# Adding the two halves of an up tile on VectorE alone, in the feed-forward stages of a two-block transformer kernel

## The reference

```python
D_MODEL, D_FF, SEQ, CONV_W = 1024, 2816, 256, 3

def conv_ffn(x, w_up, conv_w, w_down):            # k = 0, 1
    h = causal_dwconv(x @ w_up, conv_w)           # 3 taps over time
    g, v = jnp.split(h, 2, axis=-1)
    return (jax.nn.silu(g) * v) @ w_down

def conv_ffn_2(v, w_in, conv_w, conv_b, w_out):   # k = 2, 3
    gate, up = jnp.split(v @ w_in, 2, axis=-1)
    hid = jax.nn.gelu(dwconv_centred(gate, conv_w, conv_b)) * up
    return hid @ w_out
```

## Time and profile before

| | us |
|---|---|
| median of 3 runs | 1357.15 |
| lowest and highest | 1355.12, 1357.15 |
| the profiled execution | 1358.22 |
| its span, first to last instruction | 1356.9 |
| its mean granted TensorE clock | 0.996 of full speed |

### The profile page before, as it was taken

The page is one execution under the profiler, slowest core; times in us unless marked ns, Lnnn a source line. Parts: engine busy times, 40 slices in busy tenths (PEclk is TensorE's granted clock), DMA queues, the critical chain, the costliest instruction groups (busy, mean ns, idle before and its releaser), DMA issues. The chain is left out here.

```text
span 1356.9 us, 20744 instructions
## 1 busy us (share of the span) xinstructions
PE 1334.4 (98%) x8197; PEld 1160.9 (86%) x8197; DVE 1023.1 (75%) x1670; ACT 785.7 (58%) x1274; POOL 145.0 (11%) x131
## 2 busy tenths in 40 slices
PE   8999999999999999999999999999999999999998
PEld 7887888888898888887987888888789998888887
DVE  5875588777897787778788677766657997786766
ACT  6654266655442566563687565555557785655553
POOL 4760300000100000000000000000303224000000
PEclk9999999999999999999999999999999999999999
DMA  8722355654563456552643255555344435355551
GB/s 304 244 85 119 111 200 217 234 188 184 194 249 125 186 188 251 195 197 101 234 147 119 112 205 199 225 196 187 135 179 153 149 138 189 146 187 205 194 197 70
DMA packets 38607, 242.18 MB, mean 178 GB/s; under 512 B 4448, under 2 KB 7408, under 8 KB 11120
## 3 DMA queue, kind: packets, MB, share of 16 engines
q1 hardware_dynamic: 38512, 240.87, 48.2%
HBM read 236.89 MB, written 2.64 MB: 177 GB/s over the span
## 5 line engine op out<-in xcount | busy, mean ns | idle before, releaser
L320 DVE TENSOR_TENSOR wlo<-raw,whi 128x2048 fp32r<-128x2048 f32 (+1 forms) x179 | 401.2, 2246 | 103.8 <-ACT whi L297 101.7
L297 ACT ACTIVATE whi<-raw 128x2048 fp32r<-128x2048 f32 x195 | 370.4, 1903 | 81.3 <-PE ps L472 40.0
L409 PE MATMUL ps<-XS,whi 128*128 128x512 f32 x1392 | 331.7, 390 | 0.0
L409 PEld LDWEIGHTS ps<-XS,whi 128*128 128x128 f32 x1392 | 257.9, 188 | 52.0 <-issue 0.6
L461 PE MATMUL ps<-whi,MS 128*128 128x512 f32 x960 | 233.5, 391 | 0.0
L461 PEld LDWEIGHTS ps<-whi,MS 128*128 128x128 f32 x960 | 177.5, 188 | 35.8 <-issue 0.4
L414 PEld LDWEIGHTS ps<-XS,wlo 128*128 128x128 f32 x1392 | 178.5, 191 | 6.8
L414 PE MATMUL ps<-XS,wlo 128*128 128x256 f32 x1392 | 180.6, 283 | 0.0
L389 PE MATMUL ps<-XS,whi 128*128 128x256 f32 x672 | 167.8, 289 | 0.0
L390 PE MATMUL ps<-XS,whi 128*128 128x256 f32 x672 | 164.1, 284 | 0.0
L1563 ACT ACTIVATE ar<-ps 128x256 f32<-128x256 f32 x176 | 57.3, 377 | 146.3 <-PE ps L414 146.1
(11 more groups left out here) (328 smaller groups left out, 1548.4 us busy)
## 6 DMA issues: line engine op xcount, KB each, us to landing
raw<-in_up SPq DMA_DIRECT2D x88, 1024.0 KB, 4.8
raw<-in_down SPq DMA_DIRECT2D x44, 1024.0 KB, 4.9
raw<-in_hg_t SPq DMA_DIRECT2D x16, 1024.0 KB, 4.8
raw<-in_od_t SPq DMA_DIRECT2D x8, 1024.0 KB, 5.2
raw<-in_ev_a SPq DMA_DIRECT2D x6, 1024.0 KB, 10.0
raw<-in_wa_o SPq DMA_DIRECT2D x6, 1024.0 KB, 4.9
raw<-in_hg_o SPq DMA_DIRECT2D x6, 1024.0 KB, 4.8
raw<-in_ev_o SPq DMA_DIRECT2D x4, 1024.0 KB, 6.8
```

The costliest lines, as they stand in the source:

```text
L297: ac.activation(parts_of(m)[0][:, 0:w], raw[m % NRAW][:, 0:w], ACT.Copy).then_inc(w_hi)
L320: ve.tensor_tensor(lo[:, c], r[:, c], hi[:, c].bitcast(F32), ALU.subtract).then_inc(w_lo_v)
L409: pe.matmul(banks[i][:, 0:512], hi[:, c], XS[:, k, 0:512], start=(k == 0), stop=False)
```

## The change

ScalarE no longer copies the low-activation half out of the banks. VectorE makes the sum by itself: for each of the two banks one `tensor_reduce` reads all 512 columns as 256 pairs (column t and column 256 + t, 1 KB apart in the bank) and writes the 256 sums to `fS`. The semaphore `f_cb` goes. VectorE waits for `w_done` itself, and from j = 3 on also for the taps of tile j-3 that ScalarE read from the same `fS` buffer.

```diff
@@ ffn_act @@
                 w = taps(k, j)
-                ac.wait_ge(w_done, DONE[t])
-                for i in range(2):
-                    b = up_banks(k, j)[i]
-                    ac.activation(o[:, 256 * i:256 * i + 256], b[:, 256:512], ACT.Copy).then_inc(f_cb.up())
                 if j:
                     silu_act(k, j - 1)
                 ac.wait_ge(f_sm.sem, 22 * k + j + 1)
@@ added_dve @@
             o = fS[j % 3]
+            ve.wait_ge(w_done, DONE[ffn_up(k, j)])
+            if j >= 3:
+                ve.wait_ge(f_in.sem, 22 * k + j - 2)
             for i in range(2):
-                ve.wait_ge(f_cb.sem, 44 * k + 2 * j + i + 1)
-                c = slice(256 * i, 256 * i + 256)
-                ins = ve.tensor_tensor(o[:, c], up_banks(k, j)[i][:, 0:256], o[:, c], ALU.add)
+                both = up_banks(k, j)[i][:, :].rearrange("p (s t) -> p t s", s=2)
+                ins = ve.tensor_reduce(o[:, 256 * i:256 * i + 256], both, AX.X, ALU.add)
             ins.then_inc(f_sm.up())
```

More of the change, by code:

```diff
@@ L1480, in program @@
         fS = [R(512) for _ in range(3)]
-        f_cb, f_sm = mark("f_cb"), mark("f_sm")
+        f_sm = mark("f_sm")
         f_in, f_ga, f_cv, f_si, f_mu = mark("f_in"), mark("f_ga"), mark("f_cv"), mark("f_si"), mark("f_mu")
```

## The result

The changed kernel takes 1364.97 us (median of 4 runs, 1363.39 to 1365.39), the kernel before 1356.52 beside it (4 runs): a ratio of 1.0061, interval [1.0048, 1.0073]. On a second occasion it was 1363.55 against 1356.63 us, 1.0054 [1.0041, 1.0066]. So it is 7 to 8.5 us slower, where 5.7 were forecast; the time was forecast at 1362.9 with a range to 1368.

A forecast was written before the change was run, and what follows sets the result against it. TensorE, busy for 98% of the span, was taken as the bound. Head losses of 2.08, 2.16, 1.22 and 0.25 us sum to 5.7, so 1357.15 + 5.7 = 1362.9 us; range 1359.6 to 1368, own range 1361 to 1364.5.

The forecast's parts named there:

- What bounds: Feed-forward stages: TensorE is busy for all of both windows, so removing ScalarE's copies and VectorE's wait for them gains zero.
- The price of a pair of reductions: VectorE's sums: a pair takes 1.29 us against 0.75 for two additions, adding 0.54 us to every up tile.
- The upper bound: Rival at VectorE's sums: every result costs a step too, adding 1.06 us a pair, 1371.2 us in all; chance 0.07.
- The closed loop and the margins: Stage heads: VectorE has no pause, so tile 3's sums come 2.16 us late; less each stage's margin, 5.7 us lost.
- The handing over: Between VectorE's sums and TensorE's up tile: 0.09 us taken as needed, anything above it counted as margin.
- The loss behind the head: Rest of each stage: VectorE needs 15.38 us for a group of 16.57, still catches up, so no further loss.
- a sign of it being wrong: Forecast wrong if waits are absent despite a 1.29 us pair, go on in the stage's rest, or the clock newly falls.
- the weights of up tile 7: Behind the head: ScalarE's weight split for this tile, next place that could be late, keeps 0.48 us to spare.
- a cheaper pair: VectorE's sums: a pair adding only 0.35 us sets the range's lower end, 1359.6; reductions about as cheap as additions: chance 0.15.
- the clock: Rival at the heads: new waits pull TensorE's clock down, 1.75 us a fall in three stages, 1368.1 us; chance 0.15.

The follow-up runs named there:

- ScalarE's load put back: The changed kernel with two copies of constants on ScalarE per up tile, behind the old wait, results unread: 1363.88 us, ratio 1.0051.
- idle work: The kernel before with one more 452-column VectorE addition from constants between each tile's two additions, result unread: 1365.6 us, ratio 1.0073.
- third reduction: The changed kernel with a third, unread reduction for up tiles 0 to 3 of each stage: 1372.41 us, ratio 1.0122.
- head by order and the old tail: The changed kernel with sums ahead of weights' low parts for tiles 1 to 5, and copies and additions again for tiles 20 and 21: 1356.18 us, ratio 1.0001.
- the sums first: The changed kernel with sums of tiles 1 to 5, and the last product, made ahead of weights' low parts: 1358.28 us, ratio 1.0011.
- head undone: The changed kernel with ScalarE copies and VectorE additions again for up tiles 0 to 5 of each stage: 1357.52 us, ratio 1.0012.
- ends undone: The changed kernel with ScalarE copies and VectorE additions again for up tiles 0 to 5, 20 and 21: 1357.48 us, ratio 1.0006.
- sums first on the kernel before: The kernel before with only VectorE's order altered, sums and last product ahead of weights' low parts: 1356.82 us, ratio 0.9995.

## Why the prediction was right, point by point

- *What bounds.* Right: TensorE had nothing to win in the stages, and the copies and VectorE's wait for them were worth nothing. The kernel with ScalarE's load put back shows it from one side, and the kernel before with idle work from the other.
- *The price of a pair of reductions.* Right: 1.28 us against the 1.29 taken over from two instructions of 512 columns. The upper bound, a step for each result, is refuted by 682 ns.
- *The closed loop and the margins.* Right in mechanism and size: 5.79 us against 5.71, in each stage within 0.2, and 15.5 against 15.3 at twice the added time. (The handing over takes 0.05 us, and not the 0.09 that was taken for it.) The forecast expected the waits view to print 5.7 us in some eight pieces; it prints 3.4 us in five, and only the lengths show the loss in full. Undoing the head takes it away.
- *The loss behind the head, put at nothing.* This failed, and by the prediction's own words a wait of TensorE behind up tile 5 was a sign of it being wrong. It checked one place behind the head, the weights of up tile 7, and of the tails only that the sums end within 0.15 us of where they did. That is right for tile 20 (0.12). But behind it the loop closes again: no pause stands ahead of the sums of tile 21, a weight split stands between its taps and its product, and TensorE has no further up tile to do. The chain had nothing to spare, a weight load already waited 0.16 us for it, and it got 0.65 later. The tails of k = 0 and 1 account for 1.3 us, and with those of k = 2 and 3 it is 1.5 us of the 7 to 8.5; undoing tiles 20 and 21 removes it from the profile. With this term the forecast would have been 1364.4 us in place of 1362.9; the measurements were 1364.97 and 1363.55. The stated range, 1359.6 to 1368, was drawn so wide for a cheaper pair and for the clock, and that it had room for the tails is luck.
- *The clock.* No fall came at the new waits: the granted clock is full over all four heads in the five profiles that have them (both of the changed kernel, idle work, third reduction, ScalarE's load back). That rival is out.
- *What is left.* 7.3 us are placed. The two measured ratios give 8.3 and 7.3; the 1 us between lies within their intervals. Small moves in mixers that the change doesn't touch come in too. One is seen in the profiles: the longest wait of VectorE for a DMA between k = 1 and k = 2 is 2.3 us before and 2.7 us after, and that stretch is 0.35 us longer. It was not followed further.
- *The price by the page.* The Trainium skill, in VectorE: DVE Perf Modes, The perf-mode tier table, gives `tensor_reduce` only the mode of one element a cycle. The trace agrees in so far as 64 columns more cost 62 ns, about 1 ns each (682 ns for 512 columns of a bank, 620 for 448 of SBUF). The same page's Rules for kernel authors call it the slowest operation of the engine; no row here bears that out, since an addition over 512 columns takes as long (683 ns, L679). A pair is dearer here because a reduction goes through 512 columns, and an addition of the two halves through 256 (417 ns), taking one from each operand.

## What to carry to other kernels

An engine that is busy for 75% of the time can still be the one that sets the pace for 20 us: look at its loop time against that of the bounding engine stretch by stretch, and at how long each result lies ready before it is used. Where that loop is closed, an added time d per step makes a loss of n x d minus the margin. Here n was the number of up tiles whose sums TensorE needs before a down tile gives it other work: four. Do that for the end of a stage as well as for its beginning, and look there at the waits of weight loads too: the one of 0.16 us in the kernel before was the sign that nothing was left to spare. And before judging such a change, look at the order on the busy engine: the low part that stood ahead of the needed sums takes 2.2 us, four times the 0.54 us that the change added.

## What the runs showed of the hardware

TensorE's granted clock falls to its lower level (1.2 GHz) at two places of this kernel, in some executions and not in others, with the same code there. (In all eleven profiles it also falls near the end.) The windows view, with the columns of the earlier trace rows; first the changed kernel around 43 us, then around 1170:

```profile
34.00:42.50 8.50, 5.17 (x44) 4.97 (x43) 8.50 (x14) 3.46 (x7) 4.96 (x4) 1.00 1.01 361
42.50:46.00 3.50, 3.50 (x20) 3.50 (x19) 2.71 (x6) 3.41 (x5) 2.28 (x2) 0.53 1.14 319
1168.95:1172.70 3.75, 3.28 (x24) 2.70 (x24) 3.66 (x8) 2.54 (x6) 0.55 (x1) 1.00 0.00 0
1172.70:1176.20 3.50, 2.88 (x25) 2.87 (x25) 2.75 (x5) 0.74 (x4) 0.55 (x1) 1.00 0.00 0
```

The kernel with head by order and the old tail, at the first place, where it has no fall:

```profile
34.00:42.50 8.50, 5.56 (x48) 5.36 (x47) 8.40 (x17) 3.94 (x6) 4.12 (x4) 1.00 1.02 368
42.50:46.00 3.50, 3.50 (x32) 3.50 (x31) 2.69 (x4) 3.41 (x7) 3.11 (x3) 1.00 1.17 291
```

And the kernel with the sums first, at the second place, with a fall:

```profile
1160.00:1166.30 6.30, 5.20 (x35) 4.04 (x34) 5.27 (x11) 3.84 (x10) 1.27 (x3) 1.00 0.09 36
1166.30:1169.80 3.50, 3.50 (x19) 3.50 (x18) 1.77 (x3) 0.00 (x0) 0.38 (x1) 0.51 0.00 0
```

In the 3.5 us behind 42.5, TensorE gets through 20 matmuls at half the clock and 32 at the full one. What stands ahead of the first place differs between the profiles: TensorE is idle ahead of L897 there. In the five profiles with a fall (before, after, head undone, ends undone, sums first on the kernel before) that idle time is 2.95 to 3.45 us, and in the six without one 2.33 to 2.94. The fall comes 0.8 to 1.4 us behind its end. From its end to the first matmul of stage k = 0 it is 122.3 us in the five and 120.7 to 120.8 in the six, so the fall costs 1.6 us. At the second place nothing of the kind was found: the gaps of TensorE ahead of it are the same in the eleven profiles (0.6 us at most), and two of them have a fall. There the kernel before and the one with the sums first take 1.5 us longer than the others between the same two matmuls.

Runs of one kernel differ by 2 to 3 us, so a single profiled execution of each kernel could have hidden a fifth of the loss here. The lengths of stages between fixed instructions are free of it: profiles that should agree in them did so within 0.15 us.
